# VectorE inverts each chunk's variance at once, and ScalarE copies the first token blocks ahead of the gate, in the recurrence of a two-block model

## The reference

```python
u, v = gelu(zu), gelu(zv)
v = layernorm(v)                                  # per token
mixed = einsum('hts,bcshd->bcthd', tril(ws), v in 4 chunks of 128) + bs
y_a = u * mixed                                   # the spatial gate
...
def step(state, inp):                             # the recurrence
    r_t, w_t, k_t, v_t, a_t, b_t = inp
    sa = einsum('bhvk,bhk->bhv', state, a_t)
    state = state * w_t + sa * b_t + v_t * k_t
    return state, einsum('bhvk,bhk->bhv', state, r_t)
...
m = mean(y); var = mean(square(y - m))            # per head and token
y = (y - m) * rsqrt(var + 64e-5) * gn_w + gn_b
y_b = (y + bonus) * g
x = x + gate1 * (concatenate([y_a, y_b]) @ w_out)
```

## Time and profile before

| | us |
|---|---|
| runs, median of three | 2402.63 |
| runs, lowest and highest | 2402.24, 2405.5 |
| profiled execution, its own time | 2390.91 |
| its span | 2389.1 |

### The profile page before, as it was taken

One profiled execution on the slowest core, in us unless ns is written; L12 is line 12 of the kernel. 1 busy time (PEld: TensorE's weight loads), 2 busy tenths in 40 slices (PEclk: granted clock), 3 DMA queues, 4 the chain that ended last, 5 costly groups with the idle time before them and its releaser, 6 DMA issues.

```text
span 2389.1 us, 34462 instructions
## 1 busy us (share of the span) xinstructions
PE 2248.4 (94%) x14680; PEld 1632.4 (68%) x14680; DVE 1223.7 (51%) x1601; ACT 803.5 (34%) x1193; POOL 374.6 (16%) x247
## 2 busy tenths in 40 slices
PE   8998998997789979999899999999999999999998
PEld 5677875322223327877677699898787669989976
DVE  5785444300000007365865598486454739938745
ACT  3533222110011105123452354243342836424424
POOL 1001001100011000000000154262100024615310
PEclk9999989999999999999999999999999999999999
DMA  7224217999999994222121123333232012233330
GB/s 298 67 87 174 95 54 285 405 421 420 418 419 420 420 380 158 89 94 83 36 71 56 59 91 100 109 105 109 106 101 76 1 53 80 96 108 107 109 112 36
DMA packets 59021, 388.77 MB, mean 163 GB/s; under 512 B 7739, under 2 KB 7867, under 8 KB 17008
## 3 DMA queue, kind: packets, MB, share of 16 engines
q1 hardware_dynamic: 52896, 375.29, 41.2%
q0 software_dynamic: 5104, 8.09, 0.9%
q10 hardware_dynamic: 864, 3.15, 0.4%
HBM read 383.13 MB, written 13.63 MB: 166 GB/s over the span
## 4 chain that ended last, share of the span: by engine, by line
PE 79%; DMA 10%; DVE 6%; ACT 2%; SPq 1%; issue 1%; POOL 0%; DVEq 0%; POOLq 0%; ACTq 0%
PE psD L3550 39%; PE psD L2652 8%; PE psA L2652 8%; DMA ring<-w_moe 7%; PE psD L1415 7%; PE psA L3550 3%; DMA arena<-w_moe 1%; PE psA L1415 1%; SPq L795 1%; PE psA L2636 1%; DVE ring_r L3149 1%; PE psA L3625 1%; PE psD L3558 1%; PE psA L3782 1%; ACT ring_r L2928 1%
## 5 line engine op out<-in xcount | busy, mean ns | idle before, releaser
L3550 PE MATMUL psD<-rounded,ring_r 128*128 128x512 f32 (+1 forms) x3192 | 762.6, 399 | 6.4 <-DVE ring_r L3149 3.2
L3550 PEld LDWEIGHTS psD<-rounded,ring_r 128*128 128x128 f32 (+1 forms) x3192 | 596.3, 188 | 167.5 <-issue 16.6
L1415 PE MATMUL psD<-ring,arena 128*32 128x512 f32 x1568 | 178.9, 599 | 33.4 <-DMA ring<-w_moe 32.7
L3149 DVE TENSOR_TENSOR ring_r<-ring,ring_r 128x2048 fp32r<-128x2048 f32 (+2 forms) x71 | 159.0, 2239 | 83.4 <-ACT ring_r L2928 81.3
L2652 PE MATMUL psD<-rounded,fast_r 128*128 128x256 f32 x1680 | 199.5, 279 | 0.0
L2652 PE MATMUL psA<-rounded,fast_r 128*128 128x256 f32 x1680 | 199.3, 279 | 0.0
L2652 PEld LDWEIGHTS psA<-rounded,fast_r 128*128 128x128 f32 x1680 | 197.8, 188 | 0.4
L2652 PEld LDWEIGHTS psD<-rounded,fast_r 128*128 128x128 f32 x1680 | 197.6, 188 | 0.1
L2928 ACT ACTIVATE ring_r<-ring 128x2048 fp32r<-128x2048 f32 (+2 forms) x71 | 131.7, 1855 | 192.8 <-PE psD L3550 172.8
L1415 PE MATMUL psD<-arena 128*32 128x512 f32 x1504 | 171.7, 596 | 24.1 <-DMA arena<-w_moe 22.0
L3550 PE MATMUL psD<-rounded,fast_r 128*128 128x512 f32 x792 | 185.4, 395 | 0.0
(11 more groups left out here) (559 smaller groups left out, 2678.9 us busy)
## 6 DMA issues: line engine op xcount, KB each, us to landing
ring<-w_dense SPq DMA_DIRECT2D x134, 1024.0 KB, 5.1
ring<-w_moe SPq DMA_DIRECT2D x49, 2048.0 KB, 34.6
arena<-w_moe SPq DMA_DIRECT2D x47, 2048.0 KB, 33.9
ring<-w_dense SPq DMA_DIRECT2D x16, 768.0 KB, 4.3
ring<-w_dense SPq DMA_DIRECT2D x16, 640.0 KB, 3.9
arena<-pair_rows SPq DMA_DIRECT2D x8, 512.0 KB, 7.8
arena<-x_t SPq DMA_DIRECT2D x1, 2048.0 KB, 8.2
token_rows<-arena ACTq DMA_DIRECT2D x4, 512.0 KB, 10.9
```

The lines of the kernel that those rows point to most:

```text
L1415: mm = pe.matmul(bank_[32 * g:32 * g + 32], rows(g), weights(g), start=start, stop=stop_)
L3149: dve.tensor_tensor(lo_, src, hi, ALU.subtract).then_inc(sem("w_lo"), 1)
L3550: mm = pe.matmul(out, w[a], x[b], start=start and i == 0, stop=stop_ and i == 2)
```

## The change

Two things move. (1) On ScalarE the Gelu of `zu` becomes a function, `spatial_gate`, and is called in round 0 behind `by_tokens(0)`, `mod_row(1, 0, 0, MROW)` and `diagonals(0)`, where it stood ahead of all of them. (2) On VectorE `scales`, the wait for the root and the reciprocal, moves from the end of the round, behind `level_6`, the next `diagonals` and `columns`, to directly behind `variance`. No instruction is added or removed.

```diff
@@ ScalarE
             root(small[:, 48:52])
-            group_ready(act, ("zu", 1))
-            for h in range(2):
-                act.activation(YC[:, 2 * h:2 * h + 2, :], dbank(("zu", h)), ACT.Gelu_apprx_tanh)\
-                   .then_inc(group_freed(("zu", h)), 1)
+            def spatial_gate():
+                group_ready(act, ("zu", 1))
+                for h in range(2):
+                    act.activation(YC[:, 2 * h:2 * h + 2, :], dbank(("zu", h)), ACT.Gelu_apprx_tanh)\
+                       .then_inc(group_freed(("zu", h)), 1)
+
...
             for d in range(NCH + 1):
+                if d == 0:
+                    by_tokens(d)
+                    mod_row(1, 0, 0, MROW)
                 if d < NCH:
                     diagonals(d)
...
                 if d == 0:
-                    by_tokens(d)
-                    mod_row(1, 0, 0, MROW)
+                    spatial_gate()
                 halfway_5(d)
@@ VectorE
                 if d > 0:
-                    asked_at = variance(d - 1)
+                    scales(d - 1, variance(d - 1))
...
                 columns(d, 1)
                 if d > 0:
-                    scales(d - 1, asked_at)
                     normed(d - 1)
```

## The result

| | us |
|---|---|
| before, 11 executions: median (lowest to highest) | 2396.83 (2387.0 to 2405.5) |
| changed, 11 executions: median (lowest to highest) | 2377.31 (2375.07 to 2389.18) |
| ratio changed to before, 95% interval | 0.9922 (0.9904 to 0.994) |
| profiled execution, changed: time, span, mean clock | 2377.75, 2376.0, 0.986 |
| profiled execution, before: time, span, mean clock | 2390.91, 2389.1, 0.981 |

The change makes the kernel 0.8% faster, 18.7 us by the ratio, where the forecast had 12. The median of 2377.31 lies outside the range of 2386 to 2398.

A forecast was written before the change was run, and what follows sets the result against it. TensorE's queue bounds the recurrence, so its idle places, one per round, count. 3.05 + 2.02 + 3.28 + 3.5 = 11.85, say 12 us, off the median 2402.6 gave 2390.6 us; range 2386 to 2398.

The forecast's parts named there:

- Round 0, 3.05 us: ScalarE's new order lets VectorE's last mask and mix_tokens come 3.05 us sooner; the moved Gelu has 3 us of slack.
- The table load: ScalarE's function-set switch: 1.28 us load in the trace without drain, where the skill page adds 1380 ns of drain.
- the sum by the page: Whole gain with the skill page's price for the table load, drain included: 11 us, round 1 gaining 0.4 instead of 1.4.
- Rounds 1 and 2, 2.02 and 3.28 us: TensorE's idle before group_scales goes (1.41, 1.66 us) and full clock returns 0.61 and 1.62 us.
- Round 3, 3.5 us: Earlier normed and cut start the first w_out product near 310.8 instead of 314.30; idle of some 3.5 us remains.
- It reaches the end: The recurrence's earlier end moves the experts' weights' start at 372.00, and all behind it, by the same amount.
- I take the difference and not the level: Subtracts the profile's gain from the runs' median, 11.7 us above the profiled execution: 2402.6 - 12 = 2390.6.
- rival (c): Round 1 or 2 enters u0 at low clock and stays there: gain of 1 us, 2401.5, chance 0.08.
- the 9.6 us of idle time: Gain over all four rounds if the clock gives nothing back: 3.05 + 1.41 + 1.66 + 3.5.
- the clock's term: Filled idle keeps TensorE's clock up, giving back 0.61 us in round 1 and 1.62 in round 2, none in round 3.
- theory C: Experiments' theory: the excess gain comes from TensorE's clock in the recurrence, as removed idle stretches start its 1.2 GHz periods.
- rival (d): Low clock held in both rounds 1 and 2: 7.4 us slower, 2410, chance 0.04; small products kept round 3 low.

The follow-up runs named there:

- e8: Changed kernel with VectorE's cut of the first w_out unit ahead of normed(2) in round 3; median 2381.05 us, 0.9939 of before.
- e1: The kernel before, unchanged, run again; median 2393.43 us, ratio 1.0001; its profiled execution took 2403.16 us.
- e6: The changed kernel, unchanged, run again; median 2383.26 us, 0.9937 of before.
- e10: The changed kernel, unchanged, run a third time; median 2384.5 us, 0.9948 of before.
- e9: Only VectorE's part of the change on the kernel before, run again; median 2381.84 us, 0.9937 of before.
- e3: Only VectorE's part of the change on the kernel before; median 2380.8 us, 0.9938 of before.
- e7: Changed kernel with 3 unread products of ones in TensorE's round 3 idle ahead of the first w_out product; median 2378.24 us, 0.993 of before.
- e12: Changed kernel with w_out's cut ahead of normed(2), one product of ones before w_out and the masked products' gap filled; median 2374.47 us, 0.9921 of before.
- e5: Kernel before with 1, 1 and 4 unread products of ones in TensorE's waits for the reciprocal, rounds 1 to 3; median 2389.51 us, ratio 0.9975.
- e2: Only ScalarE's part of the change on the kernel before; median 2396.98 us, 1.0007 of before.

## Why the prediction was wrong, point by point

- **Round 0, 3.05 us.** Right in this profile. `mix_tokens` starts at 196.85 (196.9 was forecast), 3.09 us sooner; the waits between the masks shrank to 0.34 and 0.24. The Gelu ends at 195.64 with 3.0 us of slack, as said.
- **The table load.** The root of round 1 follows the load at once (VectorE starts `level_6` at 231.68, 0.14 us behind the reciprocal), and round 1 gained its 1.41. The Gelu starts 0.01 us behind its own load (192.41 + 1.28, 193.70), and that load 0.02 us behind the diagonals (190.69 + 1.70). The drain that the Trainium skill adds to the load (ScalarE: Activation LUTs, What ACT_TABLE_LOAD costs) shows in neither place. The recurrence ended 11.37 us sooner, midway between the sum by the page and the one by the rows, so that number decides nothing between them; the starts behind the loads do.
- **Rounds 1 and 2, 2.02 and 3.28 us.** Right between the profiles: L3899 takes 1.10 and the second L3785 1.14 us in both, with no idle before the first.
- **Round 3, 3.5 us.** Right: an idle of 3.38 us ahead of `w_out`, ended by the cut, the first product at 302.15, and half clock behind it for some 8 us. The prediction ends `u0` at 310.5 by the low clock and at 307.3, without saying so, by the full one; only the second leaves an idle of 3.5 us. The profile has the second, with the half clock coming in the idle, at about 300.5 us; e8 has the first. From start to start all four rounds gave 0.5 us less than said: 332.57 to 321.20 is 11.37, not 11.85.
- **It reaches the end.** Right, and 1.7 us more behind it. Most of that is clock in the router, which follows at 367 us: the same four products take 1.72 us in the chain (L3561), where they took 3.23 (L3558).
- **The step that failed** is "I take the difference and not the level". It assumed that the profiled execution of before stood for the median one, with a constant between them, and so that the difference between two profiles is the difference between the medians. It isn't constant. The profile is 11.7 us below the median because the three executions that gave the median were slow ones (the median of the 75 is only 2.9 us above the profile), and by e1's profile and the clocks of the 75 such executions have TensorE at 1.2 GHz for longer. In e1 that went the way of rival (c). That rival was right in its mechanism and put on the wrong side: it was given 0.08 for the changed kernel and nothing for the kernel before, where e1 shows it (20 us at half clock over `u0`, `sa` and `y` of round 1). So two terms were off. The start, the median of three executions, was 8.8 us above that of the 75 (2402.6 against 2393.8). And the gain was too small: over the 75 executions of before and the 26 of the changed kernel the means are 2395.6 and 2380.6 us, 15.0 apart (19.0 in the first comparison, 13.4 and 13.3 for e6 and e10 beside their own runs of before). With the 9.6 us of idle time taken off, some 5.4 us are left, where the clock's term had 2.2 of the 11.85. That the 5.4 are the clock of the recurrence is argued and not shown: it is a remainder, and part of it may lie behind 372 us, as e1 and e9 show. The profile's own level less the sum, 2390.91 - 11.85 = 2379.1, would have been 1.8 us off, in part by luck: e6 and e10, the same kernel, have medians of 2383.3 and 2384.5.
- **Why the clock gave back more than its term** stays open. VectorE's part does raise the mean clock, from 0.974 to 0.984 in before to 0.984 to 0.987 in e3 and e9. That it does so by taking away idle time is what the prediction and theory C assumed; e7, e8 and e12 have the clock fall with no idle before it. Nor do rows here bear out what rival (d) says of small products keeping the clock low in round 3: products of `w_out` ran in that stretch too.
- **What could have been seen.** The clock rows of the one trace already had the half clock twice broken off just before `u0`, and once held through it for 14 us; and the three times of before (2402 to 2405) all lay 11 to 15 us above the profile. Both spoke for a profile that is not the typical execution.

## What to carry to other kernels

Where the time of the same kernel spreads by more than its timer does, compare the mean clock of the executions before a profile is taken for typical; here 0.001 of mean clock went with 2.3 us. Taking away waits of 1.4 to 3.8 us on TensorE gave some 15 us where the waits and their rows in the profile gave 8.8, so such a wait can be worth more than its length; by which way, the runs leave open. And a part that shortens the chain, like ScalarE's here, can measure as nothing while its 3 us are plain between two profiles at full clock.

## What was not expected of the hardware

TensorE stayed at 1.2 GHz while its queue was full: 16.45 of 17.00 us busy at 0.50 in e5, 20.27 of 21.00 at 0.52 in e7, 24.42 of 25.00 at 0.52 in e2. It also fell there with no idle before it: in e8 behind some 29 us of unbroken work at 1.00. Over the run of `w_out` products from 345 us to 357 every profile has 1.00. And the same program on the same chip fell into such a stretch in some executions and not in others (2376.53 to 2391.03 us in e10). What tips it is not known from these runs.
